# Three first norms worked inside the router ahead of them, and the norms behind the scans inside the convolution stages, in a two-layer hybrid backbone kernel

## What is computed

```
hl = modulate(rmsnorm(xl, norm1_g[l]), sh1, sc1)      # "norm1"; hc likewise for the context
y_da = diff_attention(...)   ; y_da = rmsnorm per head * subln_g * (1 - lam_init)
y_ml = mlstm_mixer(...)      ; y_ml = rmsnorm per head * ml_norm_g * sigmoid(o)
y_cv = bg * conv3(cg * xv, w)
m = g_da*(y_da@w_da) + g_ml*(y_ml@w_ml) + g_cv*(y_cv@w_cv);  x = x + g1 * (m @ w_o)
h = modulate(rmsnorm(x, norm2_g[l]), sh2, sc2)
q = h @ wq; s = q . keys; top 16 of both halves; top 16 of their sums -> 128 experts a token
x = x + g2 * sum_k gate_k * gelu(u_tab[e_k] . h) * v_tab[e_k]
```

## Time and profile before

| what | before |
|---|---|
| median of 3 runs | 5401.15 us (5400.7 to 5401.28) |
| the profiled execution's own time | 5397.62 us |
| its span in the trace | 5395.6 us |
| mean granted PE clock | 0.862 |
| PE / DVE / ACT / POOL busy | 73% / 51% / 32% / 27% |
| read and written in HBM | 1690.46 MB, 17.92 MB, 317 GB/s over the span |

### The profile page before, as it was taken

The page is one execution under the profiler, slowest core; times in us unless marked ns, Lnnn a source line. Parts: engine busy times, 40 slices in busy tenths (PEclk is TensorE's granted clock), DMA queues, the critical chain, the costliest instruction groups (busy, mean ns, idle before and its releaser), DMA issues.

```text
span 5395.6 us, 62657 instructions
## 1 busy us (share of the span) xinstructions
PE 3965.2 (73%) x21784; PEld 2366.6 (44%) x21784; DVE 2774.3 (51%) x6649; ACT 1727.8 (32%) x4735; POOL 1477.2 (27%) x1295
## 2 busy tenths in 40 slices
PE   6998497989987787667466666897567897655555
PEld 4676364656664454334132234676234564311111
DVE  1323747564448545765455443434676446844444
ACT  1211227342433442333222222221335353322222
POOL 0000022222223233333344342000332233345453
PEclk8899799989998898888788888899888999877787
DMA  6346377768899899989999996225996899899998
GB/s 254 134 164 249 124 282 273 285 243 293 326 355 361 334 417 392 398 359 390 377 420 413 400 415 253 86 86 195 377 373 239 327 393 379 329 404 421 401 421 355
DMA packets 265342, 1712.60 MB, mean 317 GB/s; under 512 B 37601, under 2 KB 39233, under 8 KB 77633
## 3 DMA queue, kind: packets, MB, share of 16 engines
q0 software_dynamic: 184320, 1342.26, 62.2%
q1 hardware_dynamic: 80704, 366.33, 18.2%
HBM read 1690.46 MB, written 17.92 MB: 317 GB/s over the span
## 4 chain that ended last, share of the span: by engine, by line
PE 41%; DMA 24%; DVE 16%; ACT 5%; issue 5%; POOL 3%; DVEq 2%; ACTq 2%; PEld 2%; SPq 0%; PEldq 0%; another core or an unknown queue 0%; POOLq 0%
PE psum L494 26%; DMA arena<-in_uv,arena 20%; PE psum L871 10%; DVE arena L2183 6%; POOL arena L1226 3%; PEld psum L494 1%; PE psum L439 1%; DVE arena L2098 1%; DVE arena L2091 1%; DVE arena L2092 1%; DMA arena<-in_norm_g 1%; DMA arena<-in_w_ada 1%; ACT arena L1320 1%; DVE arena L2152 1%; PE psum L679 1%
## 5 line engine op out<-in xcount | busy, mean ns | idle before, releaser
L1226 POOL DMA_INDIRECT arena<-in_uv,arena x1280 | 1473.3, 1151 | 3884.4 <-PE psum L871 2629.3
L871 PE MATMUL psum<-arena 64*64 64x512 f32 x10240 | 1532.0, 726 | 893.5 <-ACTq L1593 804.2
L2183 DVE CUSTOM_DVE_ANT_0 arena<-arena 128x1024 f32<-128x1024 f32 x1280 | 1547.6, 1225 | 1134.7 <-DMA arena<-in_uv,arena 1065.8
L494 PE MATMUL psum<-arena 128*128 128x256 f32 (+2 forms) x8480 | 1966.0, 390 | 110.1 <-DVEq L1612 68.2
L494 PEld LDWEIGHTS psum<-arena 128*128 128x128 f32 (+1 forms) x8480 | 1619.7, 195 | 558.9 <-issue 187.7
L871 PEld LDWEIGHTS psum<-arena 64*64 64x64 f32 x10240 | 383.2, 154 | 1809.7 <-ACTq L1593 1127.8
L1586 ACT ACTIVATE arena<-arena 128x2 f32<-128x2 f32 x640 | 131.0, 205 | 1543.3 <-DVEq L2185 1504.1
L1592 ACT ACTIVATE arena<-arena 128x64 f32<-128x64 f32 x1280 | 376.2, 340 | 45.3 <-issue 1.0
L439 PE MATMUL psum<-arena 128*128 128x128 f32 (+1 forms) x680 | 121.9, 331 | 282.6 <-DVE arena L1670 116.3
L1589 ACT ACTIVATE arena<-arena 128x1 f32<-128x1 f32 x1280 | 307.5, 287 | 45.0 <-issue 0.7
L439 PEld LDWEIGHTS psum<-arena 128*128 128x128 f32 (+1 forms) x680 | 93.2, 171 | 335.8 <-issue 166.4
(11 more groups left out here) (202 smaller groups left out, 2362.8 us busy)
## 6 DMA issues: line engine op xcount, KB each, us to landing
arena<-in_w_in SPq DMA_DIRECT2D x92, 1024.0 KB
arena<-in_w_mix SPq DMA_DIRECT2D x88, 768.0 KB
arena<-in_w_ada SPq DMA_DIRECT2D x32, 1536.0 KB, 11.1
arena<-in_w_wq SPq DMA_DIRECT2D x40, 1152.0 KB
arena<-in_w_mix SPq DMA_DIRECT2D x24, 1024.0 KB
arena<-in_w_wo SPq DMA_DIRECT2D x20, 1024.0 KB
arena<-in_uv,arena POOLq DMA_INDIRECT x1280
arena<-ada_rows SPq DMA_DIRECT2D x15, 512.0 KB, 5.1
```

The source lines that it names most:

```text
L494: ins = mm(out, a, b, start=(i == 0), stop=(i == last))
L871: ins = mm(psum[o, r_ * 512:r_ * 512 + 512], DIAG[rows, c, :], RING[rows, sl, D + half * 512:D + (half + 1) * 512], start=first, stop=last ...
L1226: pool.indirect_dma_start(RING[:, sl, :], None, io["uv"], bass.IndirectOffsetOnAxis(IDX[:, t, h * TOPK + k:h * TOPK + k + 1], 0)).then_inc ...
L2183: V_.tensor_tensor_reduce(out=RING[:, sl, 0:D], in0=RING[:, sl, 0:D], in1=XT[:, u % 2, :], scale=1.0, scalar=0.0, op0=ALU.mult, op1=ALU.ad ...
```

## The change

1. `norm1` of layer 0's pairs 1 and 2 is no stage any more. It is worked inside the router of (0, pair 0): pair 1 beside head 1, pair 2 beside head 5. `norm1` of layer 1's context is worked beside head 1 of the router of (0, pair 2). SP loads the tiles one head earlier, ACT squares and takes the root after `scores(h, 1)`, DVE forms the means after the first top-16 of the head and scales (now in place, `HST` equals `XS`) after the second, PE turns and ACT modulates one tile in each of the last two steps of the head. `modulation(1)` moves there too.
2. `mln` of (0, pairs 1 and 2) and of (1, pair 2) are no stages any more. Their norm stands on DVE in `mc`, at each pair's first step of `("cg", half 0)`; PE turns and ACT copies the result before `("cg", half 1)`.
3. The attention's head norm of (1, pair 2) loses its step and barrier in `da`: it stands on DVE after the first unit of `ml_on`, and is turned in `mc` too.
4. Places of `HT`, `XS`, `HST` and `JUNK` in the arena are changed for this (`PLACE`, `GATED`; not shown). `quotas()` deals each segment's groups to the stages that are left. All arithmetic is as before.

```diff
--- before.py
+++ after.py
@@ -89,7 +89,11 @@
...
-DEFERRED = ((0, (0,)), (1, (1,)))
+DEFERRED = ((0, (0,)), (1, (1,)), (1, (2,)))
+def normed_in_mc(l, pairs):
+    return (l, pairs) not in ((0, (0,)), (1, (1,)))
@@ -131,6 +135,12 @@
 FIRST, ADA_AT = (0, (0,)), 4
+NORM_AT = {(0, (0,)): {1: (0, 1), 5: (0, 2)}, (0, (2,)): {1: (1, 0)}}
+def norm_beside(l, pairs, h):
+    return NORM_AT.get((l, pairs), {}).get(h)
@@ -143,11 +153,11 @@
...
     a = [(k, 0, (0,)) for k in ("norm1", "qkv", "da", "mlp", "ml", "mc", "mln", "merge", "route")]
-    b = [(k, 0, both) for k in ("norm1", "qkv", "da", "mlp", "ml", "mc", "mln")] + [("merge", 0, (1,)), ("route", 0, (1,))]
-    c1 = [("merge", 0, (2,)), ("route", 0, (2,))] + [(k, 1, (0,)) for k in ("norm1", "kv", "mlp", "ml")]
+    b = [(k, 0, both) for k in ("qkv", "da", "mlp", "ml", "mc")] + [("merge", 0, (1,)), ("route", 0, (1,))]
+    c1 = [("merge", 0, (2,)), ("route", 0, (2,))] + [(k, 1, (0,)) for k in ("kv", "mlp", "ml")]
...
     d = [("norm1", 1, (2,)), ("kv", 1, (2,)), ("mlp", 1, (2,)), ("edge", 1, (2,)), ("da", 1, (1,)), ("ml_back", 1, both), ("mln", 1, (1,)), ("merge", 1, (1,))]
-    e1 = [("route", 1, (1,)), ("q", 1, (2,)), ("da", 1, (2,)), ("ml_on", 1, both), ("mc", 1, (2,)), ("mln", 1, (2,)), ("merge", 1, (2,)), ("route", 1, (2,))]
+    e1 = [("route", 1, (1,)), ("q", 1, (2,)), ("da", 1, (2,)), ("ml_on", 1, both), ("mc", 1, (2,)), ("merge", 1, (2,)), ("route", 1, (2,))]
@@ -511,15 +521,18 @@
...
+            def norm_turned(l, p, i):
+                hst = buf(l, p, "HST", [2, D])
+                pe.wait_ge(s("normed"), nxt("normed"))
+                bs = fill(("n1", l, tiles_of(p)[i]), 2)
+                for k in range(KD):
+                    ins = turn(psum[:, bs[0] * 512 + k * P:bs[0] * 512 + (k + 1) * P], hst[:, i, k * P:(k + 1) * P])
+                full(ins)
             def norm1(kind, l, pairs):
                 for p in pairs:
-                    hst = buf(l, p, "HST", [2, D])
-                    for i, t in enumerate(tiles_of(p)):
-                        pe.wait_ge(s("normed"), nxt("normed"))
-                        bs = fill(("n1", l, t), 2)
-                        for k in range(KD):
-                            ins = turn(psum[:, bs[0] * 512 + k * P:bs[0] * 512 + (k + 1) * P], hst[:, i, k * P:(k + 1) * P])
-                        full(ins)
+                    for i in range(2):
+                        norm_turned(l, p, i)
@@ -736,6 +749,11 @@
...
                 for hh, name in cv_ops():
+                    if (hh, name) == (1, "cg") and normed_in_mc(l, pairs):
+                        for p in pairs:
+                            if (l, pairs) in DEFERRED:
+                                heads_turned(l, p, "day", buf(l, p, "YD", [2, W5]))
+                            heads_turned(l, p, "mly", ym_of(l, p, (l, p) == (1, 2)))
@@ -839,6 +857,7 @@
...
                 for h in range(PH):
+                    beside = norm_beside(l, pairs, h)
@@ -846,9 +865,13 @@
...
                         queries(h + 1, 1)
+                    if beside:
+                        norm_turned(*beside, 0)
...
                         scores(h + 1, 0)
+                    if beside:
+                        norm_turned(*beside, 1)
@@ -1053,7 +1076,13 @@
...
+            def ml_norm_row(l, pairs):
+                nrow = buf(l, pairs[0], "NRM", [W5])
+                sp.dma_start(nrow, io["ml_norm_g"][l:l + 1, :].to_broadcast([P, W5])).then_inc(s("nrow"), 16)
             def mc(kind, l, pairs):
+                if normed_in_mc(l, pairs):
+                    ml_norm_row(l, pairs)
@@ -1075,8 +1104,7 @@
...
             def mln(kind, l, pairs):
-                nrow = buf(l, pairs[0], "NRM", [W5])
-                sp.dma_start(nrow, io["ml_norm_g"][l:l + 1, :].to_broadcast([P, W5])).then_inc(s("nrow"), 16)
+                ml_norm_row(l, pairs)
@@ -1134,6 +1162,15 @@
             def route(kind, l, pairs):
...
                     chunks(1)
+                    if norm_beside(l, pairs, h + 1):
+                        l_, p_ = norm_beside(l, pairs, h + 1)
+                        if l_:
+                            sp.wait_ge(s("x2_stored"), 64 * (2 * p_ + 2))
+                        if (l_, p_) == (0, 2):
+                            sp.wait_ge(s("filled"), UNIT["n1", 0, tiles_of(1)[1]][1])
+                        for i, t in enumerate(tiles_of(p_)):
+                            sp.dma_start(buf(l_, p_, "XS", [2, D])[:, i, :], x_source(l_, t)).then_inc(s("xs_in"), 16)
+                            cnt["normed"] += 1
@@ -1267,23 +1304,26 @@
             def norm1(kind, l, pairs):
                 for p in pairs:
-                    st = 0 if p == 0 else 1
...
                     root(2)
-                    ht = buf(l, p, "HT", [KD, PW])
-                    for i, t in enumerate(tiles_of(p)):
-                        bs = whole(("n1", l, t))
+                    for i in range(2):
...
                             act.wait_ge(s("n1_mods"), l + 1)
-                        for k in range(KD):
-                            b = bs[k // 4]
-                            ins = A.activation(ht[:, k, i * P:(i + 1) * P], bank(b)[:, (k % 4) * P:(k % 4 + 1) * P], ACT.Identity,
-                                               bias=N1B[:, l, st, k:k + 1], scale=N1A[:, l, st, k:k + 1])
-                            if k % 4 == 3:
-                                empty(ins, b)
-                        yield
-                barrier()
+                        modulated(l, p, i)
+                        yield
+                barrier()
+            def modulated(l, p, i):
+                st = 0 if p == 0 else 1
+                ht = buf(l, p, "HT", [KD, PW])
+                bs = whole(("n1", l, tiles_of(p)[i]))
+                for k in range(KD):
+                    b = bs[k // 4]
+                    ins = A.activation(ht[:, k, i * P:(i + 1) * P], bank(b)[:, (k % 4) * P:(k % 4 + 1) * P], ACT.Identity,
+                                       bias=N1B[:, l, st, k:k + 1], scale=N1A[:, l, st, k:k + 1])
+                    if k % 4 == 3:
+                        empty(ins, b)
@@ -1438,7 +1478,7 @@
...
                         ahead(i + 1)
-                    if i == 1 and kind == "ml_back":
+                    if (kind, i) in (("ml_back", 1), ("ml_on", 0)):
@@ -1456,6 +1496,13 @@
...
                         cvs = buf(l, p, "CVS", [6, 260])
+                        if (hh, name) == (0, "cg") and normed_in_mc(l, pairs):
+                            root(8)
+                        if (hh, name, p) == (1, "cg", pairs[0]) and normed_in_mc(l, pairs):
+                            for p_ in pairs:
+                                if (l, pairs) in DEFERRED:
+                                    heads_turned(l, p_, "day", buf(l, p_, "QT", [CH, PW]))
+                                heads_turned(l, p_, "mly", buf(l, p_, "YMT", [CH, PW]))
@@ -1544,7 +1591,12 @@
...
                 for h in range(PH):
+                    beside = norm_beside(l, pairs, h)
                     scores(h, 1)
+                    if beside:
+                        act.wait_ge(s("xs_in"), nxt("xs_in", 32))
+                        squares(buf(*beside, "XS", [2, D]), buf(*beside, "JUNK", [D]))
+                        root(2)
@@ -1553,11 +1605,17 @@
...
                         queries(h + 1, 1)
+                    if beside:
+                        act.wait_ge(s("n1_mods"), beside[0] + 1)
+                        modulated(*beside, 0)
...
                         softmax(h)
+                    if beside:
+                        act.wait_ge(s("n1_mods"), beside[0] + 1)
+                        modulated(*beside, 1)
@@ -1644,22 +1702,25 @@
...
-            def roots(n, width):
+            def mean_squares(n, width):
                 TSC(MS[:, 0:n], SS[:, 0:n], 1.0 / width, EPS, ALU.mult, ALU.add).then_inc(s("ms"), 1)
+            def inverse_roots(n):
...
+            def roots(n, width):
+                mean_squares(n, width)
+                inverse_roots(n)
+            def modulation(l):
+                dve.wait_ge(s("n1_cols"), 64 * (l + 1))
+                for st in range(2):
+                    STT(N1A[:, l, st, :], N1A[:, l, st, :], 1.0, N1G[:, l, :], ALU.add, ALU.mult)
+                dve.drain().then_inc(s("n1_mods"), 1)
             def norm1(kind, l, pairs):
-                def modulation():
-                    dve.wait_ge(s("n1_cols"), 64 * (l + 1))
-                    for st in range(2):
-                        STT(N1A[:, l, st, :], N1A[:, l, st, :], 1.0, N1G[:, l, :], ALU.add, ALU.mult)
-                    dve.drain().then_inc(s("n1_mods"), 1)
-                if pairs == (0,) and l:
-                    modulation()
@@ -1672,7 +1733,7 @@
...
                     ada(1)
-                    modulation()
+                    modulation(0)
@@ -1954,10 +2015,17 @@
...
                         seen.add((l, t))
-                    if i == 1 and kind == "ml_back":
```

(41 more changed lines are left out.)

8 lines of the change are left out of this document (4 added, 4 removed).

## The result

The changed kernel takes 5322.5 us, the median of four runs (5306.5 to 5331.3). The kernel before, in runs on the same chip, takes 5401.2 us (5400.7 to 5408.7). The ratio is 0.985, with an interval of 0.982 to 0.987: 78.7 us are gone, where 74.7 were forecast. The profiled execution of the changed kernel is the fastest of its four, 5306.48 us with a span of 5304.4, so its stages add up to more gain (91.2 us) than the median shows. The runs of before spread by 8.0 us in this set and by 13 to 22 us in three later ones, those of the changed kernel by 25 and by 13.

The account below looks back on a forecast made before the run. No single resource was taken to fill the span; a chain of waits bound it. Removing 124.7 us less 50.0 coming back nets 74.7, taking 5397.6 to 5322.9, or 5327 as median; range 5303 to 5362.

Parts of the forecast that it names:

- The stages removed: Five short stages between barriers (norms and head norms of both layers) go, saving 124.7 us.
- The groups, +30.7: Nine expert groups dealt to the remaining stages of b, c1 and e1 cost 30.7 us, bounds 17.4 and 46.8.
- The first router, +4.0: Two norms beside heads 1 and 5 cost DVE 2.0 us each, scores' copy 3 us early; bounds 4 to 16.
- The second router, +5.0: Norm at head 1 of the router of (0, pair 2) costs 5 us, between 2.4 and 13.
- `mc` of layer 0, +2.2 for turns: Head norms there: DVE's work hidden, PE's 16 turns cost 2.2 us; without cover up to 15 more.
- `ml_on`, +5.9: `da_norm` in this serial DVE chain is uncovered and costs 5.9 us, bounds 2 and 7.2.
- `mc` of (1, pair 2), +2.2: PE's 16 turns cost 2.2 us, 7.5 us of DVE norm hidden; without cover up to 7.5 more.
- the same stages longer by a gather's wait at their start: Sign of a wrong forecast: host stages lengthen because idle stages no longer fill the ring; no size given.
- Rival 1: Displaced expert groups are nearly free: 5311 us, or 5305 with the three routers absorbing theirs; chance 0.16.
- Rival 2: In-order waits of DVE and ACT in the hosts partly seen, up to 42.5 us more: 5348 to 5369; chance 0.19.
- Rival 3: Slower: ACT's waits stop the gather ring, 20.8 us at each of 12 hand-overs, 250 us; chance 0.04.
- Rival 4: No change, as the removed stages were only rest for gathers; chance 0.03.

Follow-up runs that it names:

- e1: Kernel before with all stages kept, but the five stages get no expert groups, so the planner deals them to the host stages; 5389.9 us.
- e2: Changed kernel with only the first norms moved into the two routers, the head norms kept as stages of their own; 5370.4 us.
- e4: Changed kernel with each ACT modulation beside a router head done three times, each pass drained, same values; 5348.3 us.
- e3: Changed kernel with only the head norms moved, the first norms kept as stages with the buffer places of before; 5358.3 us.
- e5: Changed kernel with the mLSTM head norm's passes in the first steps of `mc`, only the gate product left in place; 5321.7 us.
- e6: Changed kernel with `da_norm` of (1, pair 2) worked in `mc` and not in `ml_on`; 5314.4 us.
- e8: Changed kernel with each merge's residual-row loads issued behind the third group of weight chunks, not ahead of the first; 5313.7 us.

## Why the prediction came out right

**The stages removed.** 124.7 us, all of it, as put.

**The groups, +30.7.** This is the term that was mis-sized: e1 measures +16.4 in the profile and +6 by the medians. Price per group was too low in c1 and in `mc` of layer 0 (7.1 us for one against 1.93; under e2's deal 2.9), and in the rest of segment b it had the wrong sign, since `mlp` lost 6.8 us with the deal. The forecast read the slope of a group from stages whose number of groups differed; it did not ask where in a stage the group's hand-over falls, and that moved up to 7 us either way.

**The first router, +4.0.** It came to +1.7 here, and to between 0.0 and 2.3 in eight other executions with the same norms. The norm costs DVE 1.8 us a pair as added; head 1's is masked by a gap of DVE that stood there before and vanishes. The heart of the step, the slack of 3 us on the scores' copy, is confirmed by the timeline and, from the other side, by e4. Two more table loads a pair were forecast, so five in all; there are three where one was. That of Sqrt for the second pair runs at 593.95, and ACT then waits for DVE until 602.06:

```profile
593.95 1.28 ACT L1297 ACT_TABLE_LOAD   x1 [0.55 <-issue]
602.06 0.20 ACT L1297 ACTIVATE arena<-arena 128x2 f32<-128x2 f32 x1 [6.82 <-DVE arena L1706]
```

So the load lies ahead of the wait and costs the root's round trip nothing. The Trainium skill, "ScalarE: Activation LUTs", section "Table sets: the hidden batching unit", would have calls of one set batched here; in this stage the trace shows no time lost to switches, at 1.28 us each, as DVE, which sets the stage, has no wait over 0.3 us behind them. The 2.66 us of the prediction stands in the Trainium skill, "ScalarE: Activation LUTs", section "What ACT_TABLE_LOAD costs", as 1283 ns of load and 1380 of drain. The trace agrees on the first; the second no run isolates.

**The second router, +5.0.** 281.45 us came out, where "near 281 at 400 GB/s" was said. The split was off, though. e1 has no norm there and takes 279.6, so the norm costs 1.9, just under the lower bound of 2.4; in eight other executions the stage takes 281.2 to 285.0, so 1.7 to 5.4. The other 3.4 came with the deal and are counted in the group term. Bytes do not explain them: e1's router moves 112.7 MB and that of before 112.2, which at 406 GB/s is 1.3 us.

**`mc` of layer 0, +2.2 for turns, and "near 154 us with PE full".** It took 159.2. The norm's own part is +2.4, near the forecast, and the rest is the group term; under e3's deal the stage took the 154 forecast. PE did get gaps, ended by DVE's closing of a unit and not by ACT's drain. The cover of 85 idle us of DVE was there, but under this deal not quite at that place in its order (e5).

**`ml_on`, +5.9.** +6.6 in the profile, +5.0 against e1, and 6.9 regained by e6: the step holds, and the bounds of 2 and 7.2 held it.

**`mc` of (1, pair 2), +2.2.** +5.1, and +3.9 against e1 (2.4 and 2.5 in two more executions). With the passes earlier (e5) the stage is 90.6 instead of 91.9 to 93.3, so 1.3 to 2.7 us of DVE's norm were seen after all.

**The account as a whole.** The norms as measured against e1 cost 2.3 + 1.9 + 2.4 + 5.0 + 3.9 = 15.5, of 19.3 forecast. From e1's span, 5390.3 - (124.7 - 21.6) + 15.5 = 5302.7; the profiled execution has 5304.4. So the account closes to 1.7 us, but as a net: against e1, `ml` of layer 0 is 6.8 us longer (116.3 against 109.6, at a granted clock of 0.84 and not 0.89) and `ml_back` 3.4, while the router of (1, pair 1) is 5.1 and merge (1, 2) 3.2 shorter, and no run says why. By the medians the split is another: the changed kernel lies 64 to 67 us under e1, where the stages give 86, so the rest costs some 20 us more there and the groups 10 less. The changed kernel's median lies 16 us over its profiled execution, that of before 3.5 over its own; the forecast carried over the 3.5. So by the stages three errors came near to cancelling: 14 us too much for the groups, 4 too much for the norms, and some 12 too little for the step from one execution to the median. The total was forecast better than its parts, and that is in part luck. Of the 23 us between the executions of the changed kernel a third to a half is in the merges; its cause is open. The forecast had named "the same stages longer by a gather's wait at their start" as what would be wrong, with no price; what e8 found is a weight chunk's wait downstream of the hosts, and before had it too.

**The rivals.** Rival 1 (5311, or 5305) gives the profiled execution, and its reason, nearly free groups, is half right. Rival 2 is seen only in small: 1.9 and not 13 us in the second router, 2.4 and not 15 in `mc`. Rival 3 asked for 6.2 us lost at each of 12 hand-overs; e4 puts some 6 us more on ACT at two of them in the second router, and that stage grows by 10.9 us and not by 2 x 20.8, so no round of gathers was paid anew. Rival 4 falls with the result.

**What stays open.** That the deal moves `mlp` is seen in four deals, but how it does so was read from one pair of waits. Why `ml` of layer 0 takes 109.6 us in e1 and e2 and 115.3 to 116.4 elsewhere is not known. What sets apart the executions of the changed kernel, in the merges and in the router of (1, pair 1) above all, is not known either. Nor was the wait at the end of merge (0, 1) looked into, 13 to 18 us of PE before its last transposes, which all versions have.

## What to carry to other kernels

Short stages between two barriers are worth their whole length less what comes back elsewhere: of 124.7 us removed here, 79 stayed. Price each piece that comes back at its place in the order of the engine that issues it, not by idle shares. Work that hides in a stage full of PE costs its full length in a serial chain (`da_norm`: 0 in `mc`, 6.9 us in `ml_on`), and moving fixed background groups can change more by where they fall than by how many there are (`mlp`: 127.9 to 139.9 us with the same work). Look also at the queue of loads at the start of a stage: an urgent load that stands behind less urgent ones costs, and moving it was worth about as much here as the best placing of one norm (10.5 us, and 11.2 in e6, by the medians).

## What the runs showed of the hardware

- A 768 KB chunk of weights issued behind three loads of 512 KB, with gathers in flight, takes 16.4 us from issue to landing in merge (0, 1), 18.9 in merge (1, 2) of another execution, and 16.5 and 15.4 in the two merges of before.
- ScalarE's table load runs ahead of the semaphore wait of the activation that needs it: at 593.95, 8.1 us before the activation at 602.06. A change of function behind a long wait costs nothing then.
- The same 688 matmuls of `mlp` take 127.7 us of busy PE at a granted clock of 0.96 and 125.6 at 0.99; of the 6.8 us between the two stages, 3.1 are one wait and 2.1 these matmuls.
